# Down products of two FFN parts as seven block products of 256 columns in place of eight

## What is computed

```
def conv_glu_ffn(xn, w_up, conv_w, conv_b, w_down):
    u = xn @ w_up                      # 1024 -> 2 x 2816
    u = causal depthwise convolution of width 3 over tokens, + conv_b
    gate, up = jnp.split(u, 2, axis=-1)
    return (jax.nn.silu(gate) * up) @ w_down   # 2816 -> 1024
h = h + conv_glu_ffn(rmsnorm(h, g), ...)
```

## Time and profile before

| | us |
|---|---|
| median of the runs before | 1094.8 |
| the profiled execution | 1094.95 |
| its span, first to last instruction | 1093.0 |
| TensorE busy (matmuls) | 1084.9 |
| VectorE busy | 724.0 |
| ScalarE busy | 517.1 |
| GpSimd busy | 28.3 |
| granted TensorE clock, mean | 0.999 |

### The profile page before, as it was taken

The page is one execution under the profiler, slowest core; times in us unless marked ns, Lnnn a source line. Parts: engine busy times, 40 slices in busy tenths (PEclk is TensorE's granted clock), DMA queues, the critical chain, the costliest instruction groups (busy, mean ns, idle before and its releaser), DMA issues.

```text
span 1093.0 us, 14386 instructions
## 1 busy us (share of the span) xinstructions
PE 1084.9 (99%) x5124; PEld 904.7 (83%) x5124; DVE 724.0 (66%) x1097; ACT 517.1 (47%) x777; POOL 28.3 (3%) x86
## 2 busy tenths in 40 slices
PE   9999999999999999999999999999999999999997
PEld 8888888888888888888888889888888888888886
DVE  7567878657774377744776978877437773477636
ACT  6456667555543144421445767444214442244554
POOL 0001111020000000000000000000000000000001
PEclk9999999999999999999999999999999999999999
DMA  8223243332233232332234321233322223223412
GB/s 322 73 58 91 56 97 71 104 116 78 97 96 117 77 96 95 97 118 78 95 104 127 101 89 59 97 107 100 116 80 98 93 99 116 77 96 96 135 58 77
DMA packets 31407, 108.14 MB, mean 99 GB/s; under 512 B 3648, under 2 KB 3648, under 8 KB 31360
## 3 DMA queue, kind: packets, MB, share of 16 engines
q1 hardware_dynamic: 30288, 105.13, 30.6%
q0 software_dynamic: 784, 1.85, 0.7%
q10 hardware_dynamic: 288, 0.53, 0.1%
HBM read 105.39 MB, written 2.11 MB: 98 GB/s over the span
## 4 chain that ended last, share of the span: by engine, by line
PE 99%; DMA 0%; ACT 0%; DVE 0%; issue 0%; DVEq 0%; ACTq 0%
PE bank L1329 31%; PE bank L1331 31%; PE bank L1330 31%; PE bank L1445 2%; PE bank L1349 1%; PE bank L1458 1%; PE bank L1644 0%; DMA gain_and_h<-in_gain_and_x 0%; PE bank L1728 0%; PE bank L1641 0%; PE bank L1386 0%; PE bank L1383 0%; PE bank L1380 0%; PE bank L1365 0%; PE bank L1355 0%; PE bank L1368 0%
## 5 line engine op out<-in xcount | busy, mean ns | idle before, releaser
L1329 PE MATMUL bank<-x_hi,w_hi 128*128 128x512 f32 x896 | 350.1, 391 | 0.0
L1331 PE MATMUL bank<-x_hi,w_lo 128*128 128x512 f32 x896 | 348.8, 389 | 0.0
L1330 PE MATMUL bank<-x_lo,w_hi 128*128 128x512 f32 x896 | 348.7, 389 | 0.0
L846 DVE TENSOR_TENSOR w_lo<-w_raw,w_hi 128x1024 fp32r<-128x1024 f32 (+1 forms) x189 | 225.6, 1196 | 44.3 <-ACT w_hi L396 44.2
L396 ACT ACTIVATE w_hi<-w_raw 128x1024 fp32r<-128x1024 f32 (+1 forms) x189 | 193.7, 1031 | 109.2 <-PE bank L1331 108.7
L1331 PEld LDWEIGHTS bank<-x_hi,w_lo 128*128 128x128 f32 x896 | 168.2, 188 | 35.2
L1329 PEld LDWEIGHTS bank<-x_hi,w_hi 128*128 128x128 f32 x896 | 168.2, 188 | 35.1 <-issue 0.4
L1330 PEld LDWEIGHTS bank<-x_lo,w_hi 128*128 128x128 f32 x896 | 168.2, 188 | 34.5
L1329 PE MATMUL bank<-g_hi,w_hi 128*128 128x512 f32 x352 | 136.9, 389 | 0.0
L1330 PE MATMUL bank<-g_lo,w_hi 128*128 128x512 f32 x352 | 136.9, 389 | 0.0
L1331 PE MATMUL bank<-g_hi,w_lo 128*128 128x512 f32 x352 | 136.9, 389 | 0.0
(11 more groups left out here) (242 smaller groups left out, 1170.8 us busy)
## 6 DMA issues: line engine op xcount, KB each, us to landing
w_raw<-in_weights SPq DMA_DIRECT2D x189, 512.0 KB, 3.5
gain_and_h<-in_xT SPq DMA_DIRECT2D x7, 256.0 KB, 6.3
o_inv<-o_rows POOLq DMA_DIRECT2D x7, 256.0 KB, 4.7
out<-emb SPq DMA_DIRECT2D x3, 512.0 KB, 3.0
p_raw<-in_pT SPq DMA_DIRECT2D x1, 1024.0 KB, 10.3
w_raw<-in_weights SPq DMA_DIRECT2D x2, 256.0 KB, 3.7
gain_b<-in_final_gain SPq DMA_DIRECT2D x1, 512.0 KB, 4.1
gain_and_h<-in_gain_and_x ACTq DMA_DIRECT2D x1, 260.0 KB, 3.7
```

The source lines that it names most:

```text
L846: dve.tensor_tensor(w_lo[s][:, 0:w], w_raw[s][:, 0:w], w_hi[s][:, 0:w].bitcast(F32), ALU.subtract).then_inc(lo_done, 1)
L1329: pe.matmul(dst, w1, m1, start=start and i == 0, stop=False)
L1330: pe.matmul(dst, w1, m0, start=False, stop=False)
L1331: last = pe.matmul(dst, w0, m1, start=False, stop=stop and i == len(parts) - 1)
```

## The change

It touches parts 0 and 1 of both layers, four down phases. The down product of a part is cut in blocks: the output in two groups of four tiles (a *quad*), the quad in tiles of even and odd number (rows), the hidden tiles in even and odd ones, the tokens in two halves of 256. A quad is then a 2 x 2 by 2 x 2 block product, and it is done with seven block products in place of eight (Winograd's form of Strassen's scheme). Each of the seven *steps* has one weight tile of 128 x 1024, either a block (A11, A12, A22) or a sum of blocks (S1 = A21 + A22, S2 = S1 - A11, S3 = A11 - A21, S4 = A12 - S2), and one *share* of the activations, a block or a difference of blocks of 256 columns, of which there are seven. A step is 24 matmuls of 256 columns. The host packs the blocks (`quads`); as many tiles are loaded as before, eight a part.

VectorE makes the sums of weight blocks (`first_sum`, S2 inside `seven_lo`, `third_sum`, `fourth_sum`; 1024 columns each) and the shares (`shares`), ScalarE and VectorE their high and low parts (`high_shares`, `low_shares`: 512 columns for an even tile, 1280 for an odd one). Results are accumulated over steps in three banks X, Z and Y and read in between: `seven_read` adds 128 x 2 x 256 to `h` behind each step. Steps 2 and 3 of the first quad are issued in two pieces, three quarters before the last tile's shares are needed and a quarter after.

In the changed up parts the splits run three units ahead (`look_of`), and the last, unrolled body has an order of its own on both engines, with the first weight sums and the first two reads between the operations of the tiles. GpSimd builds the bands once the first unit of up02 is done, SyncE loads the gain in up12 and its loop over loads is unrolled; buffers are laid out anew so that the shares share memory with `g_hi`, `g_lo`, the pooling buffers and attention's. The split of up10 ahead of its first body loses a special case (`alone`), and one split more stands ahead of up00. The core of the diff, its indentation reduced:

```diff
+SEVEN_PARTS = (0, 1)
...
+STEPS = ("A11", "S1", "S2", "A12", "S3", "S4", "A22")
+RAWS = ("A11", "A12", "A21", "A22")
+FREED_BY = {"A11": 5, "A12": 5, "A21": 5, "A22": 7}
+QUADS = 2
...
+if part in SEVEN_PARTS:
+    add(f"down{layer}{part}", QUADS * len(STEPS), KT, QUADS * len(STEPS), QUADS * len(RAWS))
+else:
+    add(f"down{layer}{part}", KT, tiles, KT)
...
+READS = (("X", 0, 0), ("Z", 1, 1), ("X", 0, 1), ("Y", 0, 0), ("X", 1, 1), ("Z", 0, 1), ("X", 1, 0))
+SHARE = {"A11": B11, "S1": T1, "S2": T2, "A12": B21, "S3": T3, "S4": B22, "A22": T4}
+INTO = {"A11": "X", "S1": "Z", "S2": "X", "A12": "Y", "S3": "X", "S4": "Z", "A22": "X"}
+BANK_OF = ({"X": 4, "Z": 5, "Y": 6}, {"X": 7, "Z": 4, "Y": 5})
+def look_of(part):
+    return LOOK + 1 if part in SEVEN_PARTS else LOOK
...
+elif step == "S1":
+    act.wait_ge(s1_done, nth)
+    src = w_sum
+elif step == "S2":
+    act.wait_ge(s2_done, nth)
+    src = w_sum
+elif step == "S3":
+    act.wait_ge(s3_done, nth)
+    src = w_raw[raw_slot(quad_raw(name, quad, "A21"))]
+else:
+    act.wait_ge(s4_done, nth)
+    src = w_sum
+act.wait_ge(unit_done, n - SLOTS + 1)
+act.activation(w_hi[slot_of(n)][:, :], src[:, :], ACT.Copy).then_inc(hi_done, 1)
...
+def high_shares(a, v):
+    act.wait_ge(t_done, 2 * a + v + nth_seven_tile(layer, part) + 1)
+    to, src = (slice(B21 * HALF, SHARES * HALF), gt[:, 3 * HALF:]) if v else (
+        slice(0, B21 * HALF), gt[:, HALF:3 * HALF])
+    act.activation(gs_hi[:, a, to], src, ACT.Copy).then_inc(ghi_done, 1)
+def seven_body(a):
+    ends = isinstance(a, int) and a == tiles // 2 - 1
+    look_hi(name, 0, a)
+    last_tap(a, 0, 0)
+    look_hi(name, 1, a)
+    silu(a, 0)
+    last_tap(a, 0, 1)
+    if ends:
+        high_shares(a, 0)
+        look_hi(name, 2, a)
+    else:
+        look_hi(name, 2, a)
+        high_shares(a, 0)
+    last_tap(a, 1, 0)
+    silu(a, 1)
+    if ends:
+        look_hi(name, 3, a)
+    last_tap(a, 1, 1)
+    if ends:
+        split_hi(PHASES[f"down{layer}{part}"][0] + 3)
+    else:
+        look_hi(name, 3, a)
+    high_shares(a, 1)
+loop(name, seven_body if part in SEVEN_PARTS else up_body)
+if part in SEVEN_PARTS:
+    n = PHASES[f"down{layer}{part}"][0]
+    for k in range(4, QUADS * len(STEPS) + look_of(part + 1)):
...
-pool.wait_ge(evac_done, result_of("wo", KT - 1))
+pool.wait_ge(unit_done, PHASES["up02"][0] + 1)
...
+def first_sum(name, quad):
+    for block in ("A21", "A22"):
+        r = quad_raw(name, quad, block)
+        dve.wait_ge(raw_in[raw_slot(r)], landed(r))
+    a21, a22 = (w_raw[raw_slot(quad_raw(name, quad, b))][:, :] for b in ("A21", "A22"))
+    n = PHASES[name][0] + len(STEPS) * quad
+    if quad:
+        dve.wait_ge(lo_done, n - 1)
+    dve.tensor_tensor(w_sum[:, :], a21, a22, ALU.add).then_inc(s1_done, 1)
+def seven_lo(n):
+    name = phase_of(n)
+    quad, at = divmod(n - PHASES[name][0], len(STEPS))
+    step = STEPS[at]
+    a11, a21 = (w_raw[raw_slot(quad_raw(name, quad, b))][:, :] for b in ("A11", "A21"))
+    src = {"S1": w_sum[:, :], "S2": w_sum[:, :], "S4": w_sum[:, :], "S3": a21}.get(step)
+    if src is None:
+        src = w_raw[raw_slot(quad_raw(name, quad, step))][:, :]
+    dve.wait_ge(hi_done, n + 1)
+    dve.tensor_tensor(w_lo[slot_of(n)][:, :], src, w_hi[slot_of(n)][:, :].bitcast(F32),
+                      ALU.subtract).then_inc(lo_done, 1)
+    if step == "S1":
+        dve.wait_ge(lo_done, n + 1)
+        dve.tensor_tensor(w_sum[:, :], w_sum[:, :], a11, ALU.subtract).then_inc(s2_done, 1)
+    if step == "S2" and quad:
+        third_sum(name, quad)
+    if step == "A12" and quad:
+        fourth_sum(name, quad)
+def third_sum(name, quad):
+    a11, a21 = (w_raw[raw_slot(quad_raw(name, quad, b))][:, :] for b in ("A11", "A21"))
+    dve.wait_ge(s1_done, combos_before(name, quad) + 1)
+    dve.tensor_tensor(a21, a11, a21, ALU.subtract).then_inc(s3_done, 1)
+def fourth_sum(name, quad):
+    dve.wait_ge(s2_done, combos_before(name, quad) + 1)
+    dve.wait_ge(lo_done, PHASES[name][0] + len(STEPS) * quad + STEPS.index("S2") + 1)
+    a12 = w_raw[raw_slot(quad_raw(name, quad, "A12"))]
+    dve.tensor_tensor(w_sum[:, :], a12[:, :], w_sum[:, :], ALU.subtract).then_inc(s4_done, 1)
+def seven_read(name, k):
+    n = PHASES[name][0]
+    quad, at = divmod(k, len(READS))
+    b, row, tokens = READS[at]
+    first = GROUP * quad + row
+    dve.wait_ge(unit_done, n + k + 1)
+    if at:
+        dve.wait_ge(evac_done, result_of(name, k - 1))
+    dst = h[:, first:first + 3:2, tokens * HALF:(tokens + 1) * HALF]
+    dve.tensor_tensor(dst, bank[BANK_OF[quad][b]][:, :].rearrange("p (m c) -> p m c", m=2), dst,
+                      ALU.add).then_inc(evac_done, 1)
...
+def seven_body(a):
+    down = f"down{layer}{part}"
+    ends = isinstance(a, int) and a == tiles // 2 - 1
+    evacuate(a, 0, 0)
+    look_lo(name, 0, a)
+    convolve(a, 0, 0)
+    evacuate(a, 0, 1)
+    look_lo(name, 1, a)
+    convolve(a, 0, 1)
+    shares(a, 0)
+    if ends:
+        first_sum(down, 0)
+    evacuate(a, 1, 0)
+    low_shares(a, 0)
+    convolve(a, 1, 0)
+    if ends:
+        look_lo(name, 2, a)
+    evacuate(a, 1, 1)
+    look_lo(name, 3 if ends else 2, a)
+    convolve(a, 1, 1)
+    if ends:
+        seven_read(down, 0)
+    shares(a, 1)
+    if ends:
+        split_lo(PHASES[down][0] + 3)
+        seven_read(down, 1)
+    else:
+        look_lo(name, 3, a)
+    low_shares(a, 1)
+def shares(a, v):
+    pair = 2 * a + v + pairs
+    nth = a + nth_seven_tile(layer, part) // 2
+    dve.wait_ge(silu_done, pair + 1)
+    dve.wait_ge(conv_done, 2 * pair + 2)
+    if v == 0:
+        dve.tensor_tensor(gt[:, 0:HALF], s32[:, HALF:], c32[:, 1, HALF:], ALU.mult).then_inc(gmul_half, 1)
+        dve.tensor_tensor(gt[:, HALF:SEQ], s32[:, 0:HALF], c32[:, 1, 0:HALF], ALU.mult).then_inc(gmul_done, 1)
+        dve.wait_ge(gmul_half, nth + 1)
+        dve.wait_ge(gmul_done, pair + 1)
+        dve.tensor_tensor(gt[:, SEQ:3 * HALF], gt[:, 0:HALF], gt[:, HALF:SEQ], ALU.subtract).then_inc(t_done, 1)
+    else:
+        dve.tensor_tensor(gt[:, 3 * HALF:5 * HALF], s32[:, :], c32[:, 1, :], ALU.mult).then_inc(gmul_done, 1)
+        dve.wait_ge(gmul_done, pair + 1)
+        dve.tensor_tensor(gt[:, 5 * HALF:7 * HALF].rearrange("p (x c) -> p x c", x=2),
+                          gt[:, 4 * HALF:5 * HALF].rearrange("p (o c) -> p o c", o=1).broadcast_to((P, 2, HALF)),
+                          gt[:, 0:4 * HALF].rearrange("p (x c) -> p x c", x=2)[:, :, 0:HALF],
+                          ALU.subtract).then_inc(pair_t, 1)
+        dve.wait_ge(pair_t, nth + 1)
+        dve.tensor_tensor(gt[:, 7 * HALF:], gt[:, 3 * HALF:4 * HALF], gt[:, 6 * HALF:7 * HALF],
+                          ALU.subtract).then_inc(t_done, 1)
+def low_shares(a, v):
+    to, src = (slice(B21 * HALF, SHARES * HALF), gt[:, 3 * HALF:]) if v else (
+        slice(0, B21 * HALF), gt[:, HALF:3 * HALF])
+    dve.wait_ge(ghi_done, 2 * a + v + pairs + 1)
+    dve.tensor_tensor(gs_lo[:, a, to], src, gs_hi[:, a, to].bitcast(F32), ALU.subtract).then_inc(glo_done, 1)
+loop(name, seven_body if part in SEVEN_PARTS else up_body)
+if part in SEVEN_PARTS:
+    down = f"down{layer}{part}"
+    n, steps = PHASES[down][0], QUADS * len(STEPS)
+    third_sum(down, 0)
+    fourth_sum(down, 0)
+    split_lo(n + 4)
+    seven_read(down, 2)
+    split_lo(n + 5)
+    seven_read(down, 3)
+    for k in range(6, steps + look_of(part + 1)):
+        split_lo(n + k)
+        if k - 2 < steps:
+            seven_read(down, k - 2)
+        if k == len(STEPS):
+            first_sum(down, 1)
+    done += tiles
...
+def product(quad, at, ks, opens, closes):
+    step = STEPS[at]
+    n = first + len(STEPS) * quad + at
+    w1, w0, at_share = w_hi[slot_of(n)], w_lo[slot_of(n)], slice(SHARE[step] * HALF, (SHARE[step] + 1) * HALF)
+    dst = bank[BANK_OF[quad][INTO[step]]]
+    odd = 0 if step in ("A11", "S1") else 1
+    if opens:
+        pe.wait_ge(lo_done, n + 1)
+        read_before = {"S2": 1, "S3": 3, "S4": 2, "A22": 5}.get(step)
+        if read_before:
+            pe.wait_ge(evac_done, result_of(name, len(READS) * quad + read_before - 1))
+        elif quad:
+            pe.wait_ge(evac_done, result_of(name, {"A11": 0, "S1": 6, "A12": 5}[step]))
+    for m in range(2):
+        for j in ks:
+            if quad == 0 and m == 0:
+                pe.wait_ge(glo_done, pairs + 2 * j + odd + 1)
+            cols = slice((GROUP * m + j) * P, (GROUP * m + j + 1) * P)
+            out = dst[:, m * HALF:(m + 1) * HALF]
+            begins = step in ("A11", "S1", "A12") and m == 0 and j == 0
+            pe.matmul(out, w1[:, cols], gs_hi[:, j, at_share], start=begins, stop=False, skip_group_check=True)
+            pe.matmul(out, w1[:, cols], gs_lo[:, j, at_share], start=False, stop=False, skip_group_check=True)
+            last = pe.matmul(out, w0[:, cols], gs_hi[:, j, at_share], start=False,
+                             stop=closes and m == 1 and j == ks[-1], skip_group_check=True)
+    if closes:
```

(50 more changed lines are left out.)

209 lines of the change are left out of this document (132 added, 77 removed).

## The result

The changed kernel takes 1108.62 us (median of 4 runs, 1107.65 to 1109.1) against 1094.84: ratio 1.0124, 95% interval 1.0107 to 1.0142. It is slower, by 13.8 us where 6.5 were forecast. The profiled execution has 1107.65 us, 12.7 more than that of before, and a span of 1105.9.

What follows compares the result with a forecast made beforehand. TensorE, busy 99% of the span, was taken as the bound. From the profiled 1094.95 us, 13.1 saved and 19.6 of stall gave 1101.45, or 1101.3 against the median; range 1096 to 1109.

Steps and rivals of the forecast that it cites:

- TensorE's term: Changed down phases: 14 steps take 40.25 us instead of 43.5, saving 13.1 us over four if TensorE never waits.
- VectorE's schedule: Last body and both quads: operations queued at trace intervals, 0.04 us hand-offs; TensorE waits before steps 2, 3, 4, 8, 9.
- The first long wait: First quad, before step 4: TensorE waits 2.5 us for low S3 and read 2, until 31.3.
- The Trainium skill's rule on the pipe that must be empty: VectorE: would make every 0.60 a 0.69, lengthening stall some 1.5 us a part, to 1107; the prediction kept the trace's interval.
- 4.9 us a part: Both quads of each changed down phase: total TensorE stall, against 3.28 saved; four times that nets +6.5 us.
- Costed at nothing: Items given no time: SP's loads, GpSimd's bands, the gain's load, the extra split ahead of up00, three units of look-ahead.
- cover of "0.3 us": Second quad's load of A22: lands at 37.5 after 3.5 us, where the first sum is due at 37.8.
- Rival 3: Second quad, first sum behind read 5: late A22 load adds 2 us a part, giving 1109.3; chance 0.05.
- rival 4: After the 2.5 us gaps the clock falls to 1.2 GHz, one step costing 2.9 us more, giving 1112.9; chance 0.02.
- the start after a wait: TensorE restarting after VectorE ends: 0.12 us in all, from 0.04 to the weight load and a 0.33 us matmul.
- Rival 1: Changed down phases: VectorE's chain is hidden, TensorE sets the time, so faster; 1081.7 with no stall; chance 0.13.

Runs made afterwards that it cites:

- Reads first: Changed kernel with VectorE's read 6 ahead of the low part of S1 and the third sum behind read 7 in the second quad: 1106.21 us, ratio 1.0097.
- load order: Changed kernel with each quad's blocks packed and loaded as A11, A21, A22, A12: 1108.27 us, ratio 1.0112.
- both orders: Changed kernel with the edits of Reads first and load order together: 1107.48 us, ratio 1.0111.
- the filled one: The both orders kernel plus 18 unused 256-column products on TensorE between steps 3 and 4 of each first quad: 1101.11 us, ratio 1.0063.
- the new order: Changed kernel with steps as A11, S1, A12, A22, S2, S4, S3, a bank for A22, sums and loads reordered: 1091.45 us, ratio to before 0.9961.
- the kernel without late sums: Changed kernel with the first quad's third and fourth weight sums left out, though its result needs them: 1099.47 us, ratio 1.0034.
- GpSimd kernel: Changed kernel with the first quad's third and fourth weight sums moved from VectorE to GpSimd: 1117.93 us, ratio 1.0205.

## Why the prediction was right and wrong

**TensorE's term** was right. Inside the steps the matmuls start 0.1199 us apart, against 0.1198 from the earlier trace rows, so the columns saved their 13.1 us.

**VectorE's schedule** was right. The table above gives 3.46 us before steps 2, 3 and 4 where 3.7 were forecast, and 0.63 and 0.53 before steps 8 and 9 (0.6 and 0.6) where the load was on time. The first long wait was forecast to end 31.3 us after the first unit of the last body is seen; in the third phase that unit is seen at 755.7, VectorE evacuates it at 758.73 (forecast 3.0 late) and step 4 starts at 786.99, 31.3 later. The intervals in unrolled code and hand-offs of 0.04 held. VectorE's busy time is 841 us, forecast 850. The Trainium skill's rule on the pipe that must be empty (VectorE: DVE Perf Modes, section The DRAIN you can't avoid) would have added 1.5 us a part to these waits, as the prediction read it; the trace after has them at or under the forecast, and agrees with what the same section adds, that a next operation which is not held starts earlier.

**The step that failed** is the total stall of "4.9 us a part", which was the chain's waits alone: the load of A22, the clock and the slow start behind each wait stood in it at nothing. In the profiled execution TensorE's lost time in the down phases is 24.4 us and not 19.6, and the whole forecast was 6.2 us short (+12.7, not +6.5), made up like this:

- "Costed at nothing", the load of A22: 2.8 us over four parts (waits before step 8 of 5.28, less 4 x 0.63). The text had seen the cover of "0.3 us" and taken 3.5 us to landing, which is the median of all loads of the kernel before. With four blocks in flight it took 5.39 us in the worst part. Rival 3 had the mechanism and its price, 2 us a part; it came in three parts at 0.3 to 1.6, and its chance of 0.05 was far too low for a cover that thin. Reads first removed the wait, load order all but 0.5 us of it.
- The clock, rival 4, chance 0.02: 1.5 us in the profiled execution, and 6 us in a kernel in which all four parts fall. It was priced at 2.9 us a fall; a fall costs 1.5, as the two kinds of phase in the kernel with both orders and the filled one show. Over the four kernels with this wait unchanged (changed, reads first, load order, both orders) it fell behind 10 of 16 waits of 2.43 to 2.45 us.
  The Trainium skill (TensorE: Matmul & The Clock Gate, section The HAM clock gate), which the prediction cites, has idleness bring the lower level back; the runs agree on that much.
- After each wait the second matmul starts 0.19 to 0.22 us after the first and not 0.12: 0.40 us a part over five waits, 1.6 us in all. The forecast had 0.12 for the start after a wait, and nothing for the second. It took this price from the earlier trace rows, where the matmul that waited has 144 columns, and set its 0.33 us against the 0.28 of 256 columns; with 256 columns it lasts 0.36.
- The tail, 0.9 us, and some 0.5 at the start and between phases. Why the tail is longer is open.
- Against it, the waits that were forecast came out 1.1 us smaller (18.5 for 19.6).

With these the 6.2 us are accounted for. A phase with the load on time and no fall is the second one of load order: 45.29 us, where the forecast's own terms give 40.25 + 4.9 = 45.15. That the filled kernel measures 1101.11 where the forecast said 1101.3 is luck: reads first took out the wait before step 8 (0.6 us a part in the forecast), and the slow starts and the tail, which the forecast had left out, made up for it. The median of the runs lies another 1.0 us over the profiled execution; one fall more or the long opening would do it, and no profile of the longer runs shows which.

**The other rivals.** The chain is not hidden with this order. Rival 1's argument, that VectorE has the time and the order is at fault, is borne out in part by the new order, which is 3.7 us faster than before with 4 us more of VectorE's work; it also needed a fourth bank and a tile of its own for the third sum, and 2.0 us of stall a part are left.

## What to carry to other kernels

A saving of matmul columns is worth what is left after the operands have been made in time; write out the engine queue that makes them, step by step, and take the steps that need no computed operand first. A cover of 0.3 us for a load that shares the queue with three others is no cover: price it with the loads in flight, not with the median. An opening that is sometimes 2 us longer is as large as the effects looked for here, so compare phase by phase. And a wait of TensorE costs more than its length: a gap of 2.4 us took another 1.5 us through the clock more often than not, so a rival with a mechanism that no row has yet shown deserves more than 0.02 when the change creates the condition for the first time.

## What was not expected of the hardware

- A two-input operation of GpSimd on 1024 columns (2.4 to 2.7 us) holds an operation of VectorE with two inputs in SBUF that has to run beside it: 512 columns took 2.52 and 2.72 us instead of 0.68 and 0.75. An evacuation with one of its inputs in PSUM was not held (0.69).
- The granted clock falls behind waits of equal length in some parts and not in others: 1 of 4, 4 of 4, 2 of 4 and 3 of 4 in four kernels; what decides it was not found. Nor does it fall at a fixed place: in both orders TensorE is back at 479.46 and the clock is still 1.00 up to 480, then 0.66 and 0.50 in the windows shown above, while in reads first it is already down from 786.3 to 786.7 (0.56 in the mean), with TensorE back at 786.71. Waits of up to 1.95 us, in the kernel without late sums, had no fall behind them in its profile, nor had the wait of 2.27 us before step 8 of the third phase of the changed kernel, nor the filled one. Behind the 2.48 us before step 8 of the GpSimd kernel's third phase there was one.
- Work that nobody reads made a kernel faster: 18 matmuls in idle time made the four phases 4.5 us shorter in the profile. The medians differ by 6.4; the other 1.9 us of the profiles' difference are the opening.
- The same opening takes 2 us more in some executions, with TensorE's matmuls of 512 columns 0.43 us apart until about 9 us in place of 0.23.
